# Delta rule: the masked blocks between diagonal blocks placed directly behind the inverse's update

## What is computed

```python
L = jnp.where(strict, jnp.einsum("bhncd,bhnsd->bhncs", kb, k)
              * jnp.exp(jnp.where(strict, diff, 0.0)), 0.0)
rhs = jnp.concatenate([v * beta[..., None], kb * jnp.exp(gc)[..., None]], axis=-1)
sol = lax.linalg.triangular_solve(eye + L, rhs, left_side=True, lower=True,
                                  unit_diagonal=True)
```

## Time and profile before

| | us |
|---|---|
| median of 3 runs | 863.17 |
| lowest, highest | 861.78, 863.21 |
| the profiled execution | 859.06 |
| its span, first to last instruction | 857.3 |
| its mean granted TensorE clock | 0.999 |
| PE busy | 838.4 (98%) |
| DVE busy | 624.9 (73%) |
| ACT busy | 510.3 (60%) |
| POOL busy | 74.8 (9%) |

### The profile page before, as it was taken

The page is one execution under the profiler, slowest core; times in us unless marked ns, Lnnn a source line. Parts: engine busy times, 40 slices in busy tenths (PEclk is TensorE's granted clock), DMA queues, the critical chain, the costliest instruction groups (busy, mean ns, idle before and its releaser), DMA issues. The chain is left out here.

```text
span 857.3 us, 14493 instructions
## 1 busy us (share of the span) xinstructions
PE 838.4 (98%) x5726; PEld 771.0 (90%) x5726; DVE 624.9 (73%) x1130; ACT 510.3 (60%) x839; POOL 74.8 (9%) x76
## 2 busy tenths in 40 slices
PE   8999999999999999999999899999999899999996
PEld 6999999999989999999999699999899788888885
DVE  6887987998877757666665969778755466776765
ACT  6576778665377655655566877754544443645453
POOL 0100003001020211111112100230000020000000
PEclk9999999999999999999999999999999999999999
DMA  8657443457455755555555464644433243355541
GB/s 310 234 174 273 160 136 123 159 187 294 148 196 174 236 188 174 190 196 193 175 176 170 152 206 160 247 166 154 148 99 99 81 136 103 119 201 196 196 148 49
DMA packets 40587, 148.45 MB, mean 173 GB/s; under 512 B 4652, under 2 KB 5320, under 8 KB 39880
## 3 DMA queue, kind: packets, MB, share of 16 engines
q1 hardware_dynamic: 40520, 147.54, 50.8%
HBM read 146.44 MB, written 1.08 MB: 172 GB/s over the span
## 5 line engine op out<-in xcount | busy, mean ns | idle before, releaser
L1872 DVE TENSOR_TENSOR t_wl<-t_raw,t_wh 128x1024 fp32r<-128x1024 f32 x258 | 313.7, 1225 | 104.4 <-ACT t_wh L1303 103.2
L1303 ACT ACTIVATE t_wh<-t_raw 128x1024 fp32r<-128x1024 f32 x258 | 270.8, 1058 | 107.9 <-PE bank L631 57.7
L629 PE MATMUL bank<-t_hh,t_wh 128*128 128x256 f32 x1136 | 327.9, 289 | 1.3 <-DVE t_wl L1872 1.2
L631 PE MATMUL bank<-t_hh,t_wl 128*128 128x256 f32 x1136 | 321.4, 283 | 0.0
L630 PE MATMUL bank<-t_hl,t_wh 128*128 128x256 f32 x1136 | 321.3, 283 | 0.0
L629 PEld LDWEIGHTS bank<-t_hh,t_wh 128*128 128x128 f32 x1136 | 217.6, 192 | 4.4 <-DVE t_wl L1872 2.0
L630 PEld LDWEIGHTS bank<-t_hl,t_wh 128*128 128x128 f32 x1136 | 217.7, 192 | 0.9
L631 PEld LDWEIGHTS bank<-t_hh,t_wl 128*128 128x128 f32 x1136 | 217.6, 192 | 0.0
L634 PE MATMUL bank<-t_wh,t_br 128*128 128x512 f32 x384 | 123.2, 392 | 0.0
L1887 DVE SCALAR_TENSOR_TENSOR t_arena<-bank,t_par,t_arena 128x255 f32<-128x255 f32 (+2 forms) x184 | 75.3, 475 | 45.3 <-ACT t_arena L1308 45.0
L634 PE MATMUL bank<-t_wh,t_hh 128*128 128x512 f32 x224 | 91.5, 408 | 3.2 <-DVE t_wl L1872 3.2
(11 more groups left out here) (151 smaller groups left out, 841.2 us busy)
## 6 DMA issues: line engine op xcount, KB each, us to landing
t_raw<-in_ws SPq DMA_DIRECT2D x258, 512.0 KB, 4.0
t_br<-decay SPq DMA_DIRECT2D x1, 2048.0 KB, 9.1
t_arena<-in_post SPq DMA_DIRECT2D x3, 512.0 KB, 5.1
t_arena<-gates SPq DMA_DIRECT2D x1, 1536.0 KB, 10.4
t_x<-in_xin SPq DMA_DIRECT2D x2, 512.0 KB, 4.7
t_bd<-in_bd SPq DMA_DIRECT2D x1, 1024.0 KB, 8.1
t_x<-in_xtok SPq DMA_DIRECT2D x1, 1024.0 KB, 6.4
t_arena<-in_mem SPq DMA_DIRECT2D x1, 1024.0 KB, 8.5
```

The lines of the kernel that those rows point to most:

```text
L629: e.matmul(o, wh, xh, start=first, stop=False, skip_group_check=True)
L631: return e.matmul(o, wl, xh, start=False, stop=last, skip_group_check=True)
L1303: e.activation(WH[q % NS][:, :], RAW[q % NR][:, :], ACT.Copy, bias=0.0, scale=1.0).then_inc(*hi.now(q))
L1872: e.tensor_tensor(WL[q % NS][:, :], RAW[q % NR][:, :], WH[q % NS][:, :].bitcast(F), SUB).then_inc(*lo.now(q))
```

## The change

In DVE's `dn_lane` the wait for the tick ahead of the two mask products is taken out, for both steps (n = 0: b32, n = 1: b64). The products of n = 0 are issued in tick 188, directly behind the update with inv2, instead of in tick 189; those of n = 1 in tick 191, directly behind the update with inv32, instead of in tick 192. All else stays.

```diff
                 for n, name in enumerate((32, 64)):
-                    yield from walk.until(189 + 3 * n)
                     for hf in range(2):
                         e.wait_ge(*d_dn.of(f"inv{(2, 32)[n]}1"))
                         tt(WK[0][:, hf, :, :], DL[:, hf, :, :], MASKS[f"b{name}"], MUL).then_inc(*d_dn.now("c", name, hf))
                     yield from walk.until(191 + 3 * n)
                     for hf in range(2):
                         update(f"inv{name}{hf}", hf, SUB)
```

## The result

| | us |
|---|---|
| the kernel before, median (and range) of 5 runs beside it | 861.78 (859.12 to 863.21) |
| the changed kernel, median (and range) of 5 runs | 858.77 (857.37 to 859.16) |
| ratio, with its 95% interval | 0.9962 (0.9944 to 0.998) |
| profiled execution of the changed kernel, its span, its mean granted clock | 858.77, 856.9, 0.997 |

The change makes the kernel 0.38% faster, about 3.3 us. Half of the story is in the profile of the changed kernel, the other half is in neither of the two profiles.

What follows compares the result with a forecast made beforehand. PE, busy 98% of the span, bounds the kernel, so only its idle time can be saved. One shortened wait gives 1.9 us: 859.06 to 857.2 profiled, 863.17 to 861.3 us in the median; range 859.7 to 863.3.

Steps and rivals of the forecast that it cites:

- c32 is worth nothing: Moving the b32 products from tick 189 to 188: value 0, since PE did not wait for them; at most 1.3 us.
- The pair pushes the softmax by 1.32 us: DVE, tick 191: the two c64 products ahead of the softmax work delay it by 1.32 us (1.20 to 1.45).
- The rule that was weighed there: Next DVE operation waits for an empty pipe, semaphores cost nothing extra: steps 0.69, shift 1.38, gain some 0.05 us smaller.
- The wait becomes one of about 1.5 us for t_pw; the gain is 1.9 us: PE, tick 193: the 3.25 us wait before cq64 becomes about 1.5 at the window branch's transposes; next unit 1.9 us earlier.
- Bank 1 holds by 0.2 us: ACT's tanh frees bank 1 at 678.16; PE needs it at 678.36 for the next unit's second half.
- C: Rival: stretched softmax or late bank 1 enlarges the new wait; gain 0 to 1.7 us, 861.5 to 863.2; chance 0.31.
- D: Rival: late bank 1 makes PE wait 3.2 us in gt3_1_0's second half; slower, 864.5 us; chance 0.05.
- B: Rival: the stall also costs PE clock behind it; gain 1.9 + 1.6 = 3.5 us, 859.7; chance 0.08.
- I carry the difference over unchanged: Final sum: the shown runs' median, 4.1 us above the profiled execution, keeps that difference: 863.17 - 1.9 = 861.3 us.

Runs made afterwards that it cites:

- the versions that bring PE on still further: Kernel before, with both product pairs, or only b64's, issued between their tick's two updates: ratio 0.9962 for both, 0.9944 and again 0.9936 for b64's only.
- step 64 alone: Kernel before with only the b64 products moved to tick 191, those of b32 staying in tick 189: 857.21 us, ratio 0.9956.

## Why the prediction was wrong

- *c32 is worth nothing.* Right: ratio 1.0004 alone.
- *The pair pushes the softmax by 1.32 us.* Right: 1.33. Update to c64 0.72 and two steps of 0.61, as the rows had it. The rule that was weighed there, from the Trainium skill, "VectorE: DVE Perf Modes", section "The DRAIN you can't avoid", was taken by half: the same section says that a next operation that is not held back starts earlier, and the step of 0.61 us behind an operation of 0.69 agrees with that. The dependent pair does pay, 0.72 against 0.61 us.
- *The wait becomes one of about 1.5 us for t_pw; the gain is 1.9 us.* Right: 1.42 us, and 1.86 in the timeline, 1.9 between the runs at full clock.
- *Bank 1 holds by 0.2 us.* Right, no wait there, and none in the versions that bring PE on still further. C and D did not occur: every profile with step 64 moved lists no wait of PE for ACT there.
- **The step that failed is the pricing of the stall: it was counted as a wait only, and B, which adds the clock, was given 1.6 us and a chance of 0.08.** The argument against B was that the granted clock of the one profiled execution is 1.00 behind the stall. That is true of that execution, but it was one without any dip, as 12 of the 68 runs were. In some 6 of 10 the stall costs a further 2.8 us, and the change takes that away. B's price, half clock for as long as the stall lasted, was too low as well: the clock stayed at 0.50 for 5.93 us behind 3.24 us of stall. The Trainium skill, "TensorE: Matmul & The Clock Gate", Part 1, has a gate that halves the clock after the engine idles; the runs agree with that here, with 0.50 behind 3.24 us idle.
- *"I carry the difference over unchanged."* This was the same mistake from the other side. The 4.1 us between the profiled execution (859.06) and the median of the three runs (863.17) were not an offset. 863.17 is 859.0, the time at full clock, plus about what both dips cost together (1.4 and 2.8). A difference of 0.5% between a profile and the runs of the same kernel, larger than the whole forecast, was a row to be explained. The three runs, at 861.78 to 863.21, all lie in the two groups with the longer dip. With the clock in the sum, the forecast from them would have been 863.17 - 1.9 - 2.8 = 858.5, against 858.77. That it comes so near is in part luck: both medians, 863.17 and 858.77, are of executions with the dip at the start as well (the second by its profile, the first by its time), and a median of three or five runs that fall into groups up to 4.2 us apart depends on the draw.

## What to carry to other kernels

Where the engine at the limit is PE, a stall can cost more than its length: here those of 2 us and more also cost, in a share of the executions, half clock for some us behind them. So look at several executions' granted clock before pricing one, and compare the fastest runs and the medians separately; when runs fall into groups, count the groups on both sides, since a group that the change has nothing to do with can fall unevenly. If a wait of PE can't be shortened, filling it with matmuls that nobody reads can give the clock back (1.8 us here, of the 3.3 that the change is worth). And an instruction that comes too late belongs into a gap in which its engine waits anyway, not merely earlier in the queue: directly behind the update it pushed the next thing that PE needs by its own length, in front of the second update it cost nothing.

## What was not expected of the hardware

- With one and the same stall of 3.24 us the clock fell in some executions and not in others: full through it in the profile of before, 0.50 for 5.93 us behind it in another. Behind 6.35 us idle all six runs are long.
- A stall of 2.02 us was enough for a fall in one execution. Behind the one of 1.42 us the clock is 1.00 in all three profiles that have it, and of the 29 runs of the changed kernel and of step 64 alone none is above 859.16 us.
- Filling 3.03 us of idle time with matmuls whose results are overwritten made the kernel 0.2% faster, without moving its fastest run.
